# Prompt rows finished inside the experts' loop: a decoder step on one core

## The reference

```python
def rmsnorm(x, g):
    y = xf * lax.rsqrt(jnp.mean(xf * xf, axis=-1, keepdims=True) + EPS)
    return (y * g.astype(jnp.float32)).astype(x.dtype)
def hier_moe(h, ...):
    ...
    hid = (jax.nn.silu(a) * b * gates[:, :, None]).astype(t.dtype)
    out = jnp.einsum('tef,efd->td', hid, w_down)
x = x + g2[:, None, :] * hier_moe(h2, ...)
y_prompt = rmsnorm(xp, final_norm_g)
y_sample = rmsnorm(xs, final_norm_g)
```

## Time and profile before

| | us |
|---|---|
| median of 3 runs | 1165.52 (1165.39 to 1166.51) |
| profiled execution, its own time | 1166.91 |
| its span, first to last instruction | 1165.1 |
| scatter of tile 1 starts / of tile 39, the last | 739.52 / 1102.24 |
| mean granted TensorE clock | 0.974 |

### The profile page before, as it was taken

How to read it: one execution, slowest core, us unless ns; L and a number is a source line. 1 busy time by engine, 2 the same in 40 slices (tenths; PEclk the granted TensorE clock), 3 DMA queues, 4 the chain that set the end, 5 groups by cost and what they waited for, 6 DMA issues and landing times. The chain is left out here.

```text
span 1165.1 us, 18015 instructions
## 1 busy us (share of the span) xinstructions
PE 1075.8 (92%) x5413; PEld 806.9 (69%) x5414; DVE 765.8 (66%) x1256; ACT 516.1 (44%) x732; POOL 312.9 (27%) x370
## 2 busy tenths in 40 slices
PE   3799999999797989999999989999999999999992
PEld 2357777776465668787787646888888788888860
DVE  5557475747579954378887788555777555555375
ACT  5134252422333225446665243544566455544373
POOL 0046272626141000030000003333334433333244
PEclk9799999999989999999999999999999999999996
DMA  9933656567774459386766557897799877775597
GB/s 281 316 109 101 190 158 198 154 180 246 222 156 162 137 160 250 148 226 215 248 222 217 163 217 253 238 294 216 216 272 271 219 212 220 222 208 113 111 358 306
DMA packets 165460, 244.75 MB, mean 210 GB/s; under 512 B 65327, under 2 KB 122831, under 8 KB 161255
## 3 DMA queue, kind: packets, MB, share of 16 engines
q1 hardware_dynamic: 135065, 167.54, 45.0%
q0 software_dynamic: 17040, 57.87, 19.0%
q10 hardware_dynamic: 13302, 18.66, 4.6%
HBM read 169.36 MB, written 75.84 MB: 210 GB/s over the span
## 5 line engine op out<-in xcount | busy, mean ns | idle before, releaser
L126 PE MATMUL experts_psGU<-weights_we_hi,experts_x_hi 128*128 (+1 forms) x344 | 141.2, 410 | 2.1 <-DVE experts_x_lo L2714 1.0
L128 PE MATMUL experts_psGU<-weights_we_lo,experts_x_hi 128*128 (+1 forms) x344 | 136.0, 395 | 0.0
L127 PE MATMUL experts_psGU<-weights_we_hi,experts_x_lo 128*128 (+1 forms) x344 | 136.0, 395 | 0.0
L2540 POOL DMA_INDIRECT acc_d<-experts_o_sb,experts_to_col x40 | 71.0, 1776 | 209.2 <-DMA acc_d<-experts_o_sb,experts_to_col 109.5
L126 PE MATMUL front_psM<-front_hT_hi,front_w_hi 128*128 128x512 f32 x256 | 106.7, 417 | 0.9 <-DVE front_hT_lo L1043 0.9
L127 PE MATMUL front_psM<-front_hT_hi,front_w_lo 128*128 128x512 f32 x256 | 101.7, 397 | 0.0
L2733 DVE TENSOR_TENSOR experts_o_sb<-experts_psD,experts_g2r 128x1024 f32<-128x1024 f32 x43 | 52.7, 1225 | 74.5 <-PE experts_psD L128 74.5
L128 PE MATMUL front_psM<-front_hT_lo,front_w_hi 128*128 128x512 f32 x256 | 101.2, 395 | 0.0
L126 PEld LDWEIGHTS experts_psGU<-weights_we_hi,experts_x_hi 128*128 128x128 f32 x344 | 64.7, 188 | 20.9 <-issue 6.4
L128 PEld LDWEIGHTS experts_psGU<-weights_we_lo,experts_x_hi 128*128 128x128 f32 x344 | 64.6, 188 | 15.7
L2704 DVE TENSOR_TENSOR weights_we_lo<-weights_we_raw,weights_we_hi (+1 forms) x64 | 75.5, 1220 | 0.0
(11 more groups left out here) (530 smaller groups left out, 2522.3 us busy)
## 6 DMA issues: line engine op xcount, KB each, us to landing
front_raw<-in_w_ada SPq DMA_DIRECT2D x24, 1024.0 KB, 14.2
weights_we_raw<-in_exp_w_gate SPq DMA_DIRECT2D x16, 1024.0 KB
weights_we_raw<-in_exp_w_up SPq DMA_DIRECT2D x16, 1024.0 KB
weights_wd_raw<-in_exp_w_down SPq DMA_DIRECT2D x16, 1024.0 KB
front_xraw<-in_x_prompt SPq DMA_DIRECT2D x4, 2048.0 KB, 10.9
part_d<-middle_ev ACTq DMA_DIRECT2D x16, 512.0 KB, 3.8
middle_xt<-in_x_prompt SPq DMA_DIRECT2D x16, 512.0 KB, 4.8
middle_part<-part_d SPq DMA_DIRECT2D x16, 512.0 KB, 5.6
```

The lines of the kernel that those rows point to most:

```text
L126: pe.matmul(out, l_hi, r_hi, start=start, stop=False)
L127: pe.matmul(out, l_lo, r_hi, start=False, stop=False)
L128: return pe.matmul(out, l_hi, r_lo, start=False, stop=stop)
L2540: pool.indirect_dma_start(acc_d, bass.IndirectOffsetOnAxis(tc[:, u, :], 0), osb[:, u, :], None, compute_op=ALU.add).then_inc(added, 16)
```

## The change

Every prompt row is finished in the tile in which its second expert output arrives, instead of in the ending.

In `routing`, the gate of a pair that is its row's second (by expert order) is made negative by nine small POOL operations, and DVE waits for them once; after the sort, DVE derives from the sign a mask `R.last` and takes the absolute value of the gate. At the head of `experts` POOL builds `R.rows`, four row numbers per place: the row of `h2_d` to gather, the row of `acc_d` to add into (out of range for a last pair), the row of `acc_d` to read (out of range for any other pair), and the row of `y_prompt` to store. Rows out of range are left out of the transfer.

In the loop, POOL's step T gathers tile T, and for t = T-4 issues two accumulating DMAs, the scatter of osb into `acc_d` and a gather that adds rows of `acc_d` into `osb`; then it stores the finished rows of t-2, waits for last step's DMAs, copies the four index columns of tile T+1, waits until ACT has the mean square of tile t, and raises it to the power -0.5. ACT's step s gets a Square with sum and an addition of eps for tile s-2. DVE's step s gets a refinement of the root (three 128x1 operations) and the normalization of 128x1024 for tile s-3, before `out(s-1)`.

In the ending, the reads of 2048 rows, their norms, the 16 stores and the matmuls that marked the late rows are gone; the sums of the late rows move from PE to DVE and POOL.

```diff
+            def sums(t, u):
                 pool.wait_ge(oev, OEV0 + t + 1)
...
                     pool.wait_ge(added, 16 * t)
                     pool.sem_inc(freed, 1)
...
+                pool.indirect_dma_start(acc_d, bass.IndirectOffsetOnAxis(W.cols[:, u, 1:2], 0), osb[:, u, :], None,
+                                        bounds_check=TOK - 1, oob_is_err=False, compute_op=ALU.add).then_inc(added, 16)
+                pool.indirect_dma_start(osb[:, u, :], None, acc_d, bass.IndirectOffsetOnAxis(W.cols[:, u, 2:3], 0),
+                                        bounds_check=TP - 1, oob_is_err=False, compute_op=ALU.add).then_inc(acc_in[u], 16)
+            def power(t, u):
+                pool.wait_ge(mean_ok, MEAN0 + t)
+                pool.sem_inc(fence, 1)
+                pool.tensor_tensor(fss[:, u, 2:3], fss[:, u, 1:2], half[:], ALU.pow).then_inc(powers, 1)
+            def store(t, u, to):
+                pool.wait_ge(normed, NORM0 + t + 3)
+                pool.sem_inc(fence, 1)
+                pool.indirect_dma_start(y_p, bass.IndirectOffsetOnAxis(to, 0), fo[:, u, :], None,
+                                        bounds_check=TP - 1, oob_is_err=False).then_inc(y_out[u], 16)
...
             with pool.Fori(6, last + 1, 2) as t:
                 for d in range(2):
+                    pool.wait_ge(W.ic_ok, t + d + 1)
                     pool.wait_ge(xt_ps, t + d - 1)
-                    W.gather(pool, R, h2_d, t + d, d)
-                    scatter(t + d - 4, d)
+                    W.gather(pool, h2_d, t + d, d)
+                    sums(t + d - 4, d)
+                    store(t + d - 6, d, W.cols[:, d, 3:4])
+                    n, v = t + d - 1, 1 - d
+                    pool.wait_ge(xg_in[v], 8 * n + 16 - 8 * v)
+                    pool.wait_ge(acc_in[v], 8 * (n - 4) - 8 * v + 16 + ACC0)
+                    pool.wait_ge(y_out[v], 8 * (n - 6) - 8 * v + 16 + YOUT0)
+                    W.columns(pool, R, n + 2, v)
+                    power(t + d - 4, d)
...
+            def row_squares(t, u):
+                act.wait_ge(acc_in[u], 8 * t - 8 * u + 16 + ACC0)
+                act.wait_ge(fsq, FSQ0 + t + 2)
+                act.wait_ge(normed, NORM0 + t + 1)
+                act.activation(junk[:], osb[:, u, :], ACT.Square, scale=1.0 / 32, accum_out=fss[:, u, 0:1]).then_inc(fsq, 1)
+                act.wait_ge(fsq, FSQ0 + t + 3)
+                act.activation(fss[:, u, 1:2], fss[:, u, 0:1], ACT.Identity, bias=eps[:]).then_inc(mean_ok, 1)
...
                     hidden_lo(s - 1)
                     x_lo_of(s + 1, 1 - u)
+                    root_step(s - 3, 1 - u)
                     hidden(s, u)
+                    row_norm(s - 3, 1 - u)
                     out(s - 1, 1 - u)
```

More of the change, by code:

```diff
@@ L2094 @@
 NCOL = 52
+NIDX = 4
+FAR = 8192
+TINY = 1.1754944e-38
 SLOT_TILES = ((0, 2), (2, 6), (6, 11), (11, 15), (15, 17))
@@ L2313, in route_dve @@
             cp(R.gate[:], psS[:, NCOL:2 * NCOL])
+            ts(R.last[:], R.gate[:], 0.0, None, ALU.is_lt)
+            ch.link(dve.scalar_tensor_tensor(out=R.gate[:], in0=R.gate[:], scalar=-1.0, in1=R.gate[:], op0=ALU.mult, op1=ALU.max))
             dve.wait_ge(flag_mm, 1)
@@ L2422, in experts @@
         SHARED = [(1, 0), (2, 0), (2, 1)]
-        PAIR = 2 * D * 4
-        homes = [(n, i * PAIR) for n in ("we_raw", "we_hi") for i in range(ROW_PAIRS // 2)]
-        rows = [k.over(f"rows{g}", [P, 2, D], homes[g][0], F32, homes[g][1]) for g in range(ROW_PAIRS)]
+        g2s = k.over("g2s", [TS, D], "we_raw")
         fix = k.over("late_rows", [P, LATE, D], "wd_raw")
@@ L2506, in expert_sp @@
                     W.load(sp, a, e + 2)
-            sp.wait_ge(F.rows_in, 32)
+            sp.wait_ge(W.wlo, 4 * (NE - 1))
+            sp.dma_start(g2s[:], mod_d[1:ROWS, 5 * D:6 * D].unsqueeze(1).broadcast_to([NSEQ, LSEQ, D])).then_inc(s_in, 16)
             last = last_tile(sp)
-            sp.wait_ge(bulk_go, 1)
-            for g in range(ROW_PAIRS):
-                if g in FREE:
-                    sp.wait_ge(*FREE[g])
-                if g == ROW_PAIRS // 2:
-                    sp.wait_ge(gu_mm, last + 1)
-                sp.dma_start(rows[g][:], pair(acc_d[0:TP, :], g)).then_inc(px_in[g], 16)
-                if g == ROW_PAIRS // 2 + 1:
-                    sp.wait_ge(d_mm, last)
-                    sp.dma_start(xs[:], acc_d[TP:TOK, :]).then_inc(s_in, 16)
-                    sp.dma_start(x2[:], x2s_d[:, :]).then_inc(s_in, 16)
+            sp.wait_ge(samples_go, 1)
+            sp.wait_ge(d_mm, last)
+            sp.dma_start(xs[:], acc_d[TP:TOK, :]).then_inc(s_in, 16)
+            sp.dma_start(x2[:], x2s_d[:, :]).then_inc(s_in, 16)
             sp.wait_ge(s_done, 1)
@@ L2543, in expert_pool @@
             for t in range(2, 6):
+                W.columns(pool, R, t, t % 2)
+                pool.wait_ge(W.ic_ok, t + 1)
+                if t >= 4:
+                    sums(t - 4, t % 2)
                 pool.wait_ge(xt_ps, t - 1)
-                W.gather(pool, R, h2_d, t, t % 2)
+                W.gather(pool, h2_d, t, t % 2)
                 if t >= 4:
-                    scatter(t - 4, t % 2)
+                    power(t - 4, t % 2)
+                if t < 5:
+                    pool.wait_ge(xg_in[1 - t % 2], 8 * (t - 1) + 16 - 8 * (1 - t % 2))
@@ L2565, in expert_pool @@
                                         ).then_inc(late_in[d], 16)
+            store(end - 2, 0, last_to[:, 0, :])
             pool.wait_ge(late_in[0], 16)
@@ L2631, in squares @@
+            def squares(n):
+                if n == LATE_A:
+                    act.wait_ge(fsq, FSQ0 + end + 2)
+                if n < LATE_C:
+                    act.wait_ge(own_sum, n + 1)
+                elif n == LATE_C:
+                    act.wait_ge(c_sum, 1)
                 else:
                     act.wait_ge(s_x3, 1)
-                for r, x in enumerate(unit(n)):
-                    if r not in blocks:
-                        continue
-                    if n != ORDER[0] or r:
-                        act.wait_ge(sq, SQ[n] - len(unit(n)) + r)
-                    act.activation(junk[0:x.shape[0], :], x, ACT.Square, accum_out=part(n, 0)[:, r:r + 1]).then_inc(sq, 1)
+                if n:
+                    act.wait_ge(sq, n)
+                x = unit(n)
+                act.activation(junk[0:x.shape[0], :], x, ACT.Square, accum_out=part(n, 0)).then_inc(sq, 1)
@@ L2846, in expert_dve @@
             hidden_lo(end + 2)
-            store_rows()
-            norm(0)
-            norm(1)
+            late_sums(1, psB, b_sum)
             out(end + 2, 0, osb3[:])
-            for n in ORDER[2:]:
-                if n == LATE_C:
+            dve.wait_ge(oev, OEV0 + end + 3)
+            late_sums(2, psC, c_sum)
+            for n in ORDER:
+                if n == SAMPLES:
                     sample_sum()
@@ L2929, in expert_pe @@
             turn_hidden(last, 0)
-            pe.wait_ge(flags_ok, 1)
-            for d in range(LATE):
-                mm = pe.matmul(flag_ps, of_row[:, d, :], of_col[:, d, :], start=d == 0, stop=d == LATE - 1)
-            mm.then_inc(flag_mm, 1)
             halves = [slice(c * BLK, (c + 1) * BLK) for c in range(2)]
@@ L2985, in __init__ @@
         self.gate = k.sb(st, "gate", [P, NCOL])
+        self.rows = k.at("rows", [P, NCOL, NIDX], LG_AT, I32)
+        self.last = k.at("last", [P, NCOL], LG_AT + NCOL * NIDX * 4)
+        self.far = k.at("far", [P, NCOL], LG_AT + 1088, I32)
         self.tab_ok, self.all_added = k.sem("tab_ok"), k.sem("all_added")
```

319 lines of the change are left out of this document (168 added, 151 removed).

## The result

The changed kernel takes 1290.59 us in the median of 4 runs (1287.52 to 1299.83), the kernel before 1165.45 beside it (1165.03 to 1166.51). The ratio is 1.1085, 95% interval 1.1025 to 1.1146: slower by 125 us. The forecast was 1247 with a range of 1190 to 1300.

What follows compares the result with a forecast made beforehand. PE was taken to bound the loop at 9.55 us a step, POOL's closed chain of 12.1 us to replace it. 1166.9 + 97 for the chain - 16.5 for the ending = 1247 us, range 1190 to 1300.

Steps and rivals of the forecast that it cites:

- closed chain: Loop: scatter, landing, ACT's mean, power, next gather, next scatter take 12.1 us against PE's 9.55, adding 97 us over 38 steps.
- The pair of transfers: Loop, POOL: from scatter start to landing of the accumulating gather 8.0 us, with ends of 6.1 and 14.2.
- The power: Loop, POOL: the power on 128x1 takes 0.3 us with waking up, bounds 0.2 and 0.66.
- The sum of 1261: Loop: if the added norm's SBUF contention made the power 0.66 us, 14 us more than forecast; not adopted.
- Next gather to scatter: Loop, POOL: the next gather takes 1.0 us to issue, then a gap of 0.7 to the next scatter.
- Store, columns and other waits inside the 8.0: Loop, POOL: store, index copy and other waits are hidden behind the pair's landing and cost nothing.
- DVE and ACT not the bound: Loop: DVE rises to about 8.1 us a step and ACT to 7, both fitting; becoming the bound had chance 0.02.
- Table building: Ahead of POOL's loop: some 5 us delays tile 2's gather, which lands well ahead of use; nothing, or at worst 2 us.
- The ending: After the last product: 24 us in place of 40.5, a gain of 16.5 us with bounds 12 to 20.
- Clock drops cost nothing in the loop: Loop, PE: half speed for 3.4 us loses about 1.7 us, less than the 2.55 idle, so time is unchanged.
- the long chain of the rivals: Loop: contention lengthens the chain to 14.2 us a step, 1327 us, or 1290 half way; chance 0.14 for above 1295.
- The hidden chain: Loop: landing in 6.1 us and short gaps give a 9.35 us cycle, PE stays the bound, 1150 us; chance 0.07.

Runs made afterwards that it cites:

- e11: The changed kernel without VectorE's low halves of the experts' weights from the third expert on: 1263.7 us, ratio 1.0850 to the kernel before.
- e4: The changed kernel with all indices of the accumulating gather out of range, so it moves no row: 1247.5 us, ratio 1.0717 to the kernel before.
- e3: The changed kernel without VectorE's root and norm in the loop, waits and semaphores kept: 1280.9 us, ratio 1.1009 to the kernel before.
- e12: Late square, early head gathers, late power ahead of the store (1168.0 us), now with VectorE's down split ahead of the hidden rows: 1162.8 us.
- e8: Changed kernel with late power and late square (1213.7 us), plus gathers of tiles 2 and 3 ahead of GpSimd's tables, first two scatters moved: 1207.7 us.
- e1: The changed kernel with each tile's power issued one GpSimd step later: 1237.9 us, ratio 1.0642 to the kernel before.
- e13: Late square, early head gathers, late power directly behind the scatter (1162.0 us), now with VectorE's down split ahead of the hidden rows: 1173.1 us.

## Why the prediction was right, and where it was off

The mechanism came as put: a closed chain through POOL, ACT and a landing, longer than PE's step. The terms of the step, each as the mean over the 38 steps of the trace after:

| term | forecast | measured |
|---|---|---|
| scatter's start to landing of the accumulating gather | 8.0 | 9.08 (6.1 to 13.1) |
| landing to the power's start (Square, mean) | 1.55 | 1.68 |
| power | 0.3 | 0.57 |
| to the next gather | 0.55 | 0.63 |
| gather's start to the next scatter | 1.7 | 1.57 |
| step | 12.1 | 13.54 |

- **The pair of transfers** was mis-sized most, by 1.08 of 1.44 us a step. I put the gather's issue 1.9 us after the scatter, from two rows with an issue of 1.6. In the changed kernel the scatter starts when VectorE's splits run and issues in 2.19 in the mean. That is 0.58 of the 1.08; e11 takes it away and the step falls by 0.91. The sign of it was in the earlier trace rows already, whose longest scatter took 3692 ns, and the prediction makes nothing of it. The other half is in the landing itself, which came 6.59 us after the gather's own start in place of 8.0 - 1.9 = 6.1; the 8.0 was the middle of two bounds, and e4 shows that even without the gather's rows the pair takes 7.76.
- **The power** was off by 0.27: no row had a power, and I took the copy's 0.20. Its bounds (0.2 to 0.66) held 0.57. All 40 take 566 to 591 ns, and so do the 40 of e3, which has no norm, so here it was not the norm that lengthened them: it is the operation's length. The sum of 1261 with a power of 0.66 was nearer, but for another reason. In e12 a VectorE operation does hold the power up.
- **Next gather to scatter:** 1.57 against 1.7 looks right, but 0.24 of it is issue lengthened by the splits (e11: 1.33), which the forecast did not have. That it came near is luck.
- **Store, columns and other waits inside the 8.0:** right. ACT's landing wait released every step, and the power waited 154.3 us in 33 steps.
- **DVE and ACT not the bound:** right for DVE (e3: 10 us of 125); for ACT only argued, from its busy 211 of 455 us and its idle time ahead of every Square.
- **Table building "nothing, or at worst 2 us":** wrong. Tile 1's scatter came 5.8 us later in the trace, and e8, whose edit also moves the first two scatters, took 6.1 off. The prediction took the landing as well ahead of its use; 5.4 us later and with a slower issue it was not, and the half clock behind PE's pause came on top.
- **The ending:** 19.2 us against 24 forecast; with the 3.6 us between tile 39's scatter and the last product, 8.4 us better. The last norm and the last store:

```profile
1293.18 1.28 DVE L2824 SCALAR_TENSOR_TENSOR experts_sample_rows<-experts_sample_rows,experts_ss,routing_gn 64x1024 f32<-64x1024 f32 x1
```

```profile
1294.48 0.49 SPq L2526 DMA_DIRECT2D out_y_sample<-experts_sample_rows  x1
```

  From there to the end of the span pass 3.3 us, where I had 11.7 after the last store's start (before 13.7): the sample rows end the kernel, by SP's queue, and not the indirect stores. From the last product to that norm's end pass 15.9 us, where I had 11, which gives part of it back.
- **Clock drops cost nothing in the loop:** right as far as seen. PE was granted 0.50 after gaps of 2 to 7 us, but in all 33 steps the power was released by ACT and the Square by the landing (0.02 us behind it), and no scatter stood waiting for VectorE's output, so PE was never late.

Together: 1247 + 38 x 1.44 (54.6) + 5.8 - 4.8 - 3.6 = 1299.0, the profiled execution's 1299.8. The median is 43.6 above the forecast. The profiled execution's step of 13.54 belongs to the long chain of the rivals (cycle of 13.3 and more), though the median of 1290.6 is below that rival's 1295. It sized the pair at 9.0, which is what was measured, and put this down to traffic; half of the excess was VectorE's splits instead. The chances of the cases add up to 0.99, not 1; nothing hangs on it.

The hidden chain (1150) needed a pair that lands in 6.1 us and every gap short; the quickest of the 38 pairs took 6.09 and the mean 9.08. A landing of 3.2 us by bytes alone is far from both.

## What to carry to other kernels

When a step is given a wait on an engine that works in order, write down the whole round: what stands behind the wait, who needs that, and back to what the wait needs. Where its sum is longer than the busiest engine's own share, it is the step, whatever the busy shares say. Moving the wait one step later opens one round and may close another over a double buffer, so look for the next round in the waits before blaming traffic: here the same 231.53 MB took 1290.6 and 1162.0 us, and the difference was the order of a few instructions. An operation moved off one collision may run into another (e12): after such a move look at the durations of all neighbours.

## What the runs showed of the hardware

**A GpSimd indirect DMA waits for a VectorE operation with two inputs in SBUF that is already running.** VectorE around the scatter that starts at 987.33 in the changed kernel, and that scatter:

```profile
986.62 2.29 DVE L2774 TENSOR_TENSOR weights_wd_lo<-weights_wd_raw,weights_wd_hi  x1 [0.48 <-ACT weights_wd_hi L2656]
988.83 0.42 DVE L2790 TENSOR_TENSOR experts_hT_lo<-experts_psHT,experts_hT_hi 128x256 fp32r<-128x256 f32 x1
```

```profile
987.33 3.07 POOL L2562 DMA_INDIRECT acc_d<-experts_o_sb,weights_idx_cols  x1 [0.30 <-issue]
```

The split (both inputs in SBUF) has 988.91 - 987.33 = 1.58 us left, and the scatter takes 1.48 + 1.58 = 3.06. Over the scatters of tiles 1 to 38 in all 14 traces, 532 in number, the issue took 1.6 us where no weight split had over 0.12 us left at its start, and otherwise 1.48 plus what was left, within 0.06 us in 526 of them. In the other six the split starts within some nanoseconds of the scatter, and the issue took 1.6. It is the operation that was there first that counts: splits that start after the scatter did don't lengthen it, and operations with one input in PSUM (`x_lo`, `hT_lo`) don't either. A shift of 0.1 us can make it 1.6 or 3.69. In the kernel before, 19 of 38 scatters started at most 0.06 us ahead of a split, and all 19 took 1.60 to 1.61.

GpSimd's other indirect DMAs do the same, and the added norm, which reads `osb` and `gn` in SBUF, holds them up as the splits do. Of the 520 accumulating gathers in the 13 traces that have them, 129 started while a split or a norm ran and took 1.43 to 1.50 us plus what was left of it; the other 391 took 1.55 to 1.63. The gather at 1007.24 above, with its 2.13 us, is one of the first kind, behind this norm:

```profile
1006.66 1.28 DVE L2817 SCALAR_TENSOR_TENSOR experts_fo<-experts_o_sb,experts_fss,routing_gn 128x1024 f32<-128x1024 f32 x1
```

A power that comes behind a running split ends 0.42 to 0.43 us after it (13 powers, in e1, e12 and e13).

The Trainium skill (SBUF — State Buffer, Who interferes with whom) says that VectorE and GpSimd share one pair of ports under an exclusive lock, and that a VectorE instruction with two SBUF inputs contends with a GpSimd instruction that reads SBUF; the powers agree. It also infers that a `tensor_tensor` does not hold up the writing of descriptors; here 2.29 us of one did, by up to 2.1 us, and the measurement decides.

**A gather that moves no row lands no sooner than the scatter ahead of it.** In e4 it landed 0.15 to 0.3 us behind the scatter in 21 of 38 steps and never ahead of it, 7.76 us after the scatter's start in the mean, and each row out of range still passed as a small packet.
